# A decoder layer on one core: attention's output projection ahead of the convolution's, and a modulation set summed by VectorE

## The chip, the core and the metric

The kernel runs on one core of a Trainium2 chip. Five engines work side by side and meet at semaphores: TensorE (PE: matmuls and transposes), VectorE (DVE), ScalarE (ACT), GpSimd (POOL) and SyncE (SP, which only issues DMAs here). Matmuls write into eight PSUM banks; all else lives in SBUF. The metric is the device time of one execution in microseconds, the median of the runs. All data are float32 unless a row says bf16.

## The reference

```python
def reference(x, c, ...):                      # x: 1 x 256 x 1024
    mod = silu(c) @ w_ada + b_ada              # six vectors of 1024
    shift1, scale1, gate1, shift2, scale2, gate2 = split(mod)
    h = rms_norm(x) * (1 + scale1) + shift1
    x = x + gate1 * mixer(h)
    h = rms_norm(x) * (1 + scale2) + shift2
    return x + gate2 * moe(h)                  # top 4 of 32 experts, clamped SwiGLU

def mixer(h):
    u_conv, q, k, v, g = split(h @ w_in)       # 2048, 1024, 1024, 1024, 2048 columns
    y_conv = swish(layer_norm(causal_conv31(glu(u_conv)))) @ w_conv_out + b_conv_out
    o = diff_attention(rope(rms(q)), rope(rms(k)), v)     # 8 heads, two softmaxes each
    y_attn = rms_norm(o) * (1 - lam_init) @ w_attn_out
    g_conv, g_attn = split(sigmoid(g + b_gate))
    return (g_conv * y_conv + g_attn * y_attn) @ w_o
```

## The kernel before

There is no scheduler: each engine has its own program, and the order of work is the order in which its code is written. 256 tokens are two tiles of 128, 1024 channels are eight tiles of 128.

**Projections.** Weights come as blocks of 2 MB (128 x 4096) into a ring of six slots; the list `blocks` sets their order, and SP loads block n when block n-6 has been used (`used`, line 452). TensorE projects the convolution's columns, then q and k (`proj`, line 1281, eight tiles of 8 matmuls of 512 columns), then v (four tiles). The six modulation vectors come in three sets: the first (shift1, scale1) opens the kernel; the second and third (`ADA0`, four blocks of w_ada each, `ada_rows`, line 1194, 32 matmuls a set) stand before q/k and before v. Their rows are turned into columns at line 1316 (`mod2T`), and VectorE copies them out (lines 953, 955).

**Convolution.** VectorE runs the 31 taps of eight channel tiles in pairs (`conv`, line 864: a round is one tap of both tiles of a pair, two operations of 128x256). Rounds fill the time between other work: five rounds behind each of the eight q/k tiles (`between`), 28 operations and more behind them, the last ones inside heads 0 and 1. The LayerNorm follows inside the heads: sums over channels by VectorE (lines 997, 1001), mean and variance by a matmul against ones (`MEAN_AT` = 2, `VAR_AT` = 4). ScalarE's sigmoids (line 719, head 5) and GpSimd's products (lines 562, 565) make the swish.

**Heads.** q and k tiles are transposed (line 1327) and copied out by ScalarE (line 675). Per head h TensorE does the scores (lines 1360, 1364), half a gate tile (line 1288), the transposes of head h-1's probabilities (`turn`, line 1339), the other half, and head h-1's product with v (`attend`, lines 1349 to 1351). VectorE takes maxima (line 973), ScalarE the exponentials (line 698), VectorE the differences of the two softmaxes (lines 985, 986); ScalarE copies the transposed probabilities (line 681).

**Behind the heads.** Three blocks of the convolution's output projection (`y_conv`, line 1288), the transposes of the normalised heads (`oT`, line 1406; ScalarE copies them, line 729), the fourth y_conv block, four of attention's (`y_attn`), w_o (line 1426), the router, and then the expert units: a unit is up to 32 tokens of one expert, and 47 units run here. Every block here is 16 matmuls of 256 columns.

**Banks.** Banks 0 to 3 rotate: the list `order` gives every use a number, use n lies in bank n mod 4 (`bank`), and TensorE waits until use n-4 has been read out (`fill`).

**Expert weights.** 192 chunks of 2 MB go round eleven slots. The first eleven chunks take slots that the projections and tiles give up (`SLOT_ORDER`, `load_chunk`, lines 462 to 483); each later one waits for its slot's chunk to be used by a unit. GpSimd meanwhile splits the experts' biases into three bf16 pieces (lines 550 to 555), which are ready before the first unit.

## Time and profile before

| | us |
|---|---|
| median of 3 runs (1286.76 to 1287.35) | 1286.91 |
| the profiled execution | 1286.41 |
| its span, first to last instruction | 1284.6 |
| busy: TensorE matmuls / weight loads | 1080.6 / 528.3 |
| busy: VectorE / ScalarE / GpSimd | 404.4 / 219.0 / 51.7 |
| chain that ended last: PE / DMA / SP's queue | 49% / 41% / 5% |
| read from HBM: 473 MB, over the span | 369 GB/s |

The rows further down come from two views. A timeline row is a run of equal instructions: start, time from its first start to its last end, engine, line, operation, what it writes and reads, how many, and in brackets how long the engine had been idle and what released it. float32 matmuls and transposes stand as two records each. A windows row gives the busy time of each engine in one stretch, TensorE's granted clock as a share of its full 2.4 GHz, the DMA engines' busy share and GB/s.

### The profile page before, as it was taken

The page shows a single profiled execution, that of the slowest core. Times are in us where ns is not written, and L with a number is a line of the kernel's source. Part 1 is how long each engine was busy: PE and PEld are TensorE (multiplying, and loading weights), DVE is VectorE, ACT ScalarE, POOL GpSimd, SP SyncE. Part 2 cuts the span into 40 slices and gives each one's busy share as a digit, 9 for nine tenths or more (in the row PEclk, how much of TensorE's full clock was granted, in tenths as well). Part 3 has the DMA queues.
Part 4 walks back from the last instruction along what each step waited for, and adds up shares of the span by engine and source line. Part 5 has one row for each costly group of instructions (what it writes and reads, how often), then busy time and mean ns, then how long its engine had stood idle before and what let it go on. Part 6 is the DMA issues. An engine that isn't in the chain of part 4 may idle for free.

```text
span 1284.6 us, 23431 instructions
## 1 busy us (share of the span) xinstructions
PE 1080.6 (84%) x9958; PEld 528.3 (41%) x9958; DVE 404.4 (31%) x1129; ACT 219.0 (17%) x461; POOL 51.7 (4%) x91
## 2 busy tenths in 40 slices
PE   8999999899998566669998657968669696999975
PEld 5864458788433122224443212423224242444431
DVE  1388997631232111112222111212112121232221
ACT  1111124640121000002211001201002110122110
POOL 2000000355000000000000000000000000000000
PEclk9999999999999887889999888989889898999998
DMA  9998672256879999999999999999999999599997
GB/s 328 349 371 327 239 285 92 106 181 228 325 323 427 428 427 428 427 427 429 426 429 427 427 428 427 426 425 429 428 427 429 425 429 427 241 429 428 428 426 312
DMA packets 66084, 475.81 MB, mean 370 GB/s; under 512 B 6329, under 2 KB 19966, under 8 KB 39390
## 3 DMA queue, kind: packets, MB, share of 16 engines
q1 hardware_dynamic: 62100, 471.36, 89.2%
q0 software_dynamic: 816, 1.84, 0.5%
q10 hardware_dynamic: 3098, 1.56, 0.5%
q8 instruction: 59, 0.97, 0.3%
q14 instruction: 11, 0.09, 0.0%
HBM read 473.03 MB, written 1.05 MB: 369 GB/s over the span
## 4 chain that ended last, share of the span: by engine, by line
PE 49%; DMA 41%; SPq 5%; ACT 3%; DVE 1%; another core or an unknown queue 1%; issue 1%; ACTq 0%; DVEq 0%
DMA weights<-in_w_down 27%; PE bank L1556 14%; DMA weights<-in_w_up 13%; PE bank L1288 7%; PE bank L1584 7%; PE bank L1281 6%; SPq L462 4%; PE bank L1273 2%; PE bank L1426 2%; PE bank L1498 2%; PE bank L1224 2%; PE bank L1485 1%; PE bank L1194 1%; DMA weights<-in_w_ada 1%; PE bank L1505 1%
## 5 line engine op out<-in xcount | busy, mean ns | idle before, releaser
L1556 PE MATMUL bank<-weights,buf_d 128*32 128x512 f32 x3008 | 394.6, 671 | 141.6 <-DMA weights<-in_w_up 141.6
L1556 PEld LDWEIGHTS bank<-weights,buf_d 128*32 128x32 f32 x3008 | 96.9, 117 | 405.0 <-DMA weights<-in_w_up 211.5
L1584 PE MATMUL bank<-weights,buf_d 128*32 128x256 f32 x3008 | 177.6, 382 | 42.7 <-DMA weights<-in_w_down 39.9
L1165 DVE TENSOR_SCALAR u_conv<-bank 128x256 f32<-128x256 f32 x47 | 20.0, 425 | 467.5 <-PE bank L1556 467.5
L774 ACT ACTIVATE u_conv<-u_conv 128x256 f32<-128x256 f32 x47 | 19.6, 416 | 708.5 <-DVE u_conv L1165 708.5
L1584 PEld LDWEIGHTS bank<-weights,buf_d 128*32 128x32 f32 x3008 | 90.7, 110 | 115.5 <-DMA weights<-in_w_down 51.6
L864 DVE SCALAR_TENSOR_TENSOR weights<-u_conv,weights 128x256 f32<-128x256 f32 x240 | 97.8, 481 | 0.5
L1281 PE MATMUL bank<-weights,buf_d 128*128 128x512 f32 x192 | 82.9, 594 | 0.0
L1177 DVE TENSOR_TENSOR buf_d<-bank,u_conv 128x256 f32<-128x256 f32 x47 | 20.0, 425 | 180.1 <-PE bank L1584 180.1
L774 ACT ACT_TABLE_LOAD x47 | 60.3, 1283 | 1.4 <-issue 0.5
L1288 PE MATMUL bank<-buf_d,weights 128*128 128x256 f32 x256 | 58.6, 383 | 0.0
L1498 PE MATMUL bank<-buf_d 32*128 32x256 f32 x768 | 57.7, 416 | 0.6 <-DVE buf_d L1177 0.6
L1498 PEld LDWEIGHTS bank<-buf_d 32*128 32x128 f32 x768 | 36.4, 194 | 49.0 <-issue 47.6
L1288 PE MATMUL bank<-weights 128*128 128x256 f32 x256 | 55.6, 379 | 0.0
L1281 PEld LDWEIGHTS bank<-weights,buf_d 128*128 128x128 f32 x192 | 36.4, 190 | 46.6 <-issue 46.6
L1288 PEld LDWEIGHTS bank<-weights 128*128 128x128 f32 x256 | 48.6, 190 | 6.4
L1288 PEld LDWEIGHTS bank<-buf_d,weights 128*128 128x128 f32 x256 | 47.5, 190 | 8.4 <-issue 2.6
L1485 PE MATMUL bank<-x_tok,u_conv 128*32 128x256 f32 x768 | 50.1, 380 | 0.0
L1491 PE MATMUL bank<-ident,buf_d 128*128 128x128 f32 x190 | 38.2, 308 | 0.2 <-ACT buf_d L767 0.2
L1505 PE MATMUL bank<-late,u_conv 96*32 96x256 bf16 (+1 forms) x376 | 33.7, 343 | 0.5 <-DVE buf_d L1127 0.5
L1491 PEld LDWEIGHTS bank<-ident,buf_d 128*128 128x128 f32 x190 | 29.9, 204 | 4.4 <-ACT buf_d L767 0.3
L1158 DVE TENSOR_SCALAR u_conv<-u_conv 128x128 f32<-128x128 f32 x94 | 28.3, 344 | 6.8 <-issue 1.3
(274 smaller groups left out, 799.4 us busy)
## 6 DMA issues: line engine op xcount, KB each, us to landing
weights<-in_w_up SPq DMA_DIRECT2D x128, 2048.0 KB, 35.5
weights<-in_w_down SPq DMA_DIRECT2D x64, 2048.0 KB, 39.2
weights<-in_w_in SPq DMA_DIRECT2D x10, 2048.0 KB, 15.5
weights<-in_w_ada SPq DMA_DIRECT2D x8, 2048.0 KB, 19.3
weights<-in_w_ada SPq DMA_DIRECT2D x8, 1024.0 KB, 11.3
weights<-in_w_in SPq DMA_DIRECT2D x8, 512.0 KB, 10.1
weights<-in_w_in SPq DMA_DIRECT2D x4, 1024.0 KB, 13.1
weights<-in_w_conv_out SPq DMA_DIRECT2D x2, 2048.0 KB, 11.3
```

The lines of the kernel that those rows point to most:

```text
L462: sp.dma_start(dst, src).then_inc(w_full[chunk_slot(e, j)], 16)
L774: s.activation(sg, glu, ACT.Sigmoid, scale=ALPHA).then_inc(sg_ready, 1)
L864: ins = v.scalar_tensor_tensor(acc, u_conv[:, k, w:w + T], tap(k, w), acc, ALU.mult, ALU.add)
L1158: ins = v.tensor_scalar(pickw[:, tt, :], place_s.rearrange("p a s -> p (a s)"), upos[:, tt, bass.ds(u, 1)], uwt[:, tt, bass.ds(u, 1)], ALU ...
L1281: ins = t.matmul(bank(use)[:, :], lhsT[:, k, P * tt:P * tt + P], blk(n)[:, k, :], start=(k == 0), stop=(k == KD - 1))
L1288: ins = t.matmul(bank(use)[:, T * j:T * j + T], blk(n)[:, k, at:at + P], rhs[:, k, :], start=(k == 0), stop=(k == KD - 1))
L1485: ins = t.matmul(GX[SLOTS * g:SLOTS * g + SLOTS, 0:T], pick[:, tt, :], x_tok[:, tt, T * g:T * g + T], start=(tt == 0), stop=(tt == TT - 1))
L1491: ins = t.transpose(bank_[:, at + P * r:at + P * r + P], src.rearrange("p (c r) -> p r c", r=2)[:, r, :], ident[:])
L1498: ins = t.matmul(Y[q][:, T * tt:T * tt + T], Cmb[rows, P * tt:P * tt + P], oe[rows, :], start=False, stop=True, skip_group_check=True)
L1505: t.matmul(bank_[SLOTS * g:SLOTS * g + SLOTS, 0:width], sel, rows(g), start=True, stop=False)
L1556: ins = t.matmul(UP[SLOTS * g:SLOTS * g + SLOTS, :], xgT[:, r, SLOTS * j:SLOTS * j + SLOTS], up_group(w[:, r, :], g), start=False, stop=(j ...
L1584: ins = t.matmul(DOWN[rows, 0:T], actT[:, r, at:at + SLOTS], w[:, g, r, T * q:T * q + T], start=False, stop=(h == 1 and g == 1 and r == 1))
```

## The change

The third modulation set moves. Its four w_ada blocks are now loaded behind the gate blocks, and TensorE no longer multiplies them: behind the heads VectorE multiplies each of the eight 128x2048 pieces by its value of silu(c) and adds the sum so far (`mod_product`), and TensorE sums the result over partitions with four matmuls against ones (`sum_rows`), between the third and fourth y_attn block. Its columns (`turn_rows(1)`) follow the fourth.

Behind the heads the order is now oT, y_attn, then y_conv. Gate tile h-1 stands beside head h (before: gate tile h), so that none stands in head 0 and the last comes behind the last head. The swish's sigmoids leave the heads and follow the copies of oT. A q or k tile is followed by four rounds of taps instead of five; heads 0 to 3 hold 4, 5, 5 and 3 rounds, and the LayerNorm's mean and variance move from heads 2 and 4 to heads 4 and 6. The order of blocks, chunks and slots follows. The bias row of the third set is loaded straight into its place in `modrow2`.

```diff
-MEAN_AT, VAR_AT = 2, 4
+MEAN_AT, VAR_AT = 4, 6
...
-SLOT_ORDER = (0, VALUE_SLOT, 1, HEAD_SLOT, 2, 3, CONV_SLOT, GATE_SLOT, 4, 5, SMALL_SLOT)
+SLOT_ORDER = (VALUE_SLOT, 0, 1, 2, 3, CONV_SLOT, GATE_SLOT, HEAD_SLOT, 4, 5, SMALL_SLOT)
...
         blocks += [block_of(w_in, NB * i) for i in range(4, 8)]
-        ADA0[1] = len(blocks)
-        blocks += [ada_block(8 * NB, i) for i in range(4)]
         V0 = len(blocks)
         blocks += [block_of(w_in, NB * i) for i in range(8, 10)]
         GATE0 = len(blocks)
         blocks += [block_of(w_in, NB * i) for i in range(10, 14)]
+        ADA0[1] = len(blocks)
+        blocks += [ada_block(8 * NB, i) for i in range(4)]
+        AOUT0 = len(blocks)
+        blocks += [block_of(w_attn_out, 0), block_of(w_attn_out, NB)]
         COUT0 = len(blocks)
         blocks += [block_of(w_conv_out, 0), block_of(w_conv_out, NB)]
-        AOUT0 = len(blocks)
-        blocks += [block_of(w_attn_out, 0), block_of(w_attn_out, NB)]
...
-        order += [("ada", 1)] + [("v", i) for i in range(4)] + [("mod2T", 0), ("mod2T", 1)] + [("qkT", i) for i in range(8)]
-        for h in range(HEADS + 1):
-            if h < HEADS:
-                order += [("gate", h)]
-            if h:
-                order += [("aT", h - 1), ("o", h - 1)]
+        order += [("v", i) for i in range(4)] + [("mod2T", 0)] + [("qkT", i) for i in range(8)]
+        for h in range(1, HEADS):
+            order += [("gate", h - 1), ("aT", h - 1), ("o", h - 1)]
...
-        order += [("y_conv", i) for i in range(3)] + [("oT", i) for i in range(4)] + [("y_conv", 3)]
-        order += [(name, i) for name in ("y_attn", "w_o") for i in range(4)]
+        order += [("aT", HEADS - 1), ("o", HEADS - 1), ("gate", HEADS - 1)]
+        order += [("oT", i) for i in range(4)] + [("y_attn", i) for i in range(3)] + [("ada", 1), ("y_attn", 3), ("mod2T", 1)]
+        order += [("y_conv", i) for i in range(4)] + [("w_o", i) for i in range(4)]
...
-            for gi in range(2):
-                used[ADA0[gi] + i] = (ada_done, 3 * gi + i + 1)
+            used[ADA0[0] + i] = (ada_done, i + 1)
+            used[ADA0[1] + i] = (mod_summed, 2 * i + 3)
...
-            sp.wait_ge(*used[COUT0])
+            full(sp, OT_USE + 3)
             load_chunk(0, 0)
-            full(sp, OT_USE + 3)
-            load_chunk(0, 1)
-            sp.wait_ge(*used[COUT0 + 1])
-            load_chunk(0, 2)
-            sp.wait_ge(ebias_ready, 3 * PARTS)
-            load_chunk(0, 3)
             for i in range(2):
                 sp.wait_ge(*used[AOUT0 + i])
-                load_chunk(0, 4 + i)
-            full(sp, YA_USE + 3)
+                load_chunk(0, 1 + i)
+            for i in range(2):
+                sp.wait_ge(*used[COUT0 + i])
+                load_chunk(0, 3 + i)
+            full(sp, YC_USE[3])
+            load_chunk(0, 5)
+            sp.wait_ge(mixed, 4)
             load_chunk(1, 0)
-            sp.wait_ge(mixed, 4)
+            sp.wait_ge(ebias_ready, 3 * PARTS)
             load_chunk(1, 1)
...
+                    for gi in range(2):
+                        pool.wait_ge(bank_full[M2T_USE[gi] % 4], M2T_USE[gi] // 4 + 1)
                 pool.wait_ge(in_eb, 48 * (piece + 1))
...
-            for i in range(2):
-                s.activation(gates[:, KD * i:KD * i + KD, :], gates[:, KD * i:KD * i + KD, :], ACT.Sigmoid).then_inc(gate_ready, 1)
+            keep_gate(HEADS - 1)
             for i in range(4):
                 full(act_e, OT_USE + i)
...
+            sigmoid_gates(KD)
+            act_e.wait_ge(ln_ready, 1)
+            for k in range(KD):
+                s.activation(u_conv[:, k, 0:T], conv_acc[:, k, :], ACT.Sigmoid, scale=cols[:, 8 + k:9 + k],
+                             bias=cols[:, 16 + k:17 + k]).then_inc(sw_sig, 1)
+            sigmoid_gates(0)
...
+            def mod_product(k):
+                w, seen = (blk(ADA0[1] + j // 2, 2)[:, j % 2, :] for j in (k, max(k - 1, 0)))
+                if k % 2 == 0:
+                    dve.wait_ge(blk_full[place(ADA0[1] + k // 2)], 16 * loads_before[ADA0[1] + k // 2])
+                if k:
+                    dve.wait_ge(mod_summed, k)
+                    ins = v.scalar_tensor_tensor(w, w, c_act[:, k, 0:1], seen, ALU.mult, ALU.add)
+                else:
+                    ins = v.tensor_scalar(w, w, c_act[:, 0, 0:1], None, ALU.mult)
+                ins.then_inc(mod_summed, 1)
...
-            between = ([(1, 8, 13)], [(1, 13, 18)], [(1, 18, 23)], [(1, 23, 28)], [(1, 28, TAPS), (2, 0, 2)],
-                       [(2, 2, 7)], [(2, 7, 12)], [(2, 12, 17)])
+            between = ([(1, 8, 12)], [(1, 12, 16)], [(1, 16, 20)], [(1, 20, 24)], [(1, 24, 28)],
+                       [(1, 28, TAPS), (2, 0, 1)], [(2, 1, 5)], [(2, 5, 9)])
...
-            ada_row(1)
-            conv(2, 17, TAPS)
-            conv(3, 0, 11)
+            conv(2, 9, TAPS)
+            conv(3, 0, 8)
...
-            conv(3, 11, 19)
+            conv(3, 8, 14)
...
-                if h < 2:
-                    conv(3, (19, 26)[h], (26, TAPS)[h])
+                if h < 4:
+                    conv(3, (14, 18, 23, 28)[h], (18, 23, 28, TAPS)[h])
...
+            for k in range(4):
+                mod_product(k)
+            dve.wait_ge(gate_ready, 1)
+            for i in range(4):
+                use = YA_USE[i]
+                full(dve, use)
...
+                if i < 2:
+                    mod_product(2 * i + 4)
+                    mod_product(2 * i + 5)
+                if i == 2:
+                    ada_row(1)
...
+            def sum_rows():
+                use = ADA_USE[1]
+                fill(pe, use)
+                pe.wait_ge(mod_summed, KD)
+                total = blk(ADA0[1] + 3, 2)[:, 1, :]
+                for gi in range(4):
+                    ins = t.matmul(bank(use)[32 * gi:32 * gi + 32, :], ones[:, 0:32], total[:, NB * gi:NB * gi + NB],
+                                   start=True, stop=True)
+                ins.then_inc(bank_full[use % 4], 1)
...
-                channels(gate_use(h), n, par, 1, h1T)
-                if h:
+                    gate_half(h - 1, 1)
                     attend(h - 1)
...
-            conv_out(3)
             for i in range(4):
                 pe.wait_ge(bank_free[(OT_USE + i) % 4], (OT_USE + i) // 4 + 1)
             for i in range(4):
                 if i % 2 == 0:
                     wait_block(AOUT0 + i // 2)
-                fill(pe, YA_USE + i)
+                if i == 3:
+                    sum_rows()
+                fill(pe, YA_USE[i])
                 for j in range(2):
-                    channels(YA_USE + i, AOUT0 + i // 2, i % 2, j, oT)
...
+            turn_rows(1)
+            pe.wait_ge(swish_ready, KD)
+            for i in range(4):
+                conv_out(i)
```

TensorE from the last projection tile to the first scores, before (bank numbers shown; `late` is `modrow2`, the rows of the second and third set; line 1316 turns them, line 1327 transposes q and k tiles):

```order
L1316 MATMUL bank2<-ident,late 128x128 x4
L1316 MATMUL bank3<-ident,late 128x128 x4
L1327 MATMUL bank0<-ident,weights 128x128 x4
L1327 MATMUL bank1<-ident,weights 128x128 x4
L1327 MATMUL bank2<-ident,weights 128x128 x4
L1327 MATMUL bank3<-ident,weights 128x128 x4
```

And now (line 1343 turns the rows, line 1366 transposes):

```order
L1311 MATMUL bank0<-weights,buf_d 128x512 x8
L1343 MATMUL bank1<-ident,late 128x128 x4
L1366 MATMUL bank2<-ident,weights 128x128 x4
L1366 MATMUL bank3<-ident,weights 128x128 x4
L1366 MATMUL bank0<-ident,weights 128x128 x4
L1366 MATMUL bank1<-ident,weights 128x128 x4
```

One group of turned rows is left, and the fourth transposed tile now takes its bank, bank 1; before, the third and fourth took the banks of the two groups.

TensorE from the last head on, before (line 1339 is `turn`, 1349 to 1351 `attend`, 1288 a block or gate tile, 1406 oT, 1426 w_o):

```order
L1339 MATMUL bank<-ident,weights 128x128 x3
L1349 MATMUL bank<-weights 128x128
L1350 MATMUL bank<-weights 128x128
L1351 MATMUL bank<-weights 128x128
L1288 MATMUL bank<-weights 128x256 x48
L1406 MATMUL bank<-ident,weights 128x128 x16
L1288 MATMUL bank<-weights 128x256 x80
L1426 MATMUL bank<-weights,buf_d 128x512 x32
```

And now (line 1318 is a block or gate tile, 1447 oT, 1353 `sum_rows`, 1343 the turned rows, 1472 w_o):

```order
L1378 MATMUL bank<-ident,weights 128x128 x3
L1388 MATMUL bank<-weights 128x128
L1389 MATMUL bank<-weights 128x128
L1390 MATMUL bank<-weights 128x128
L1318 MATMUL bank<-buf_d,weights 128x256 x16
L1447 MATMUL bank<-ident,weights 128x128 x16
L1318 MATMUL bank<-weights 128x256 x48
L1353 MATMUL bank<-weights 32x512 x4
L1318 MATMUL bank<-weights 128x256 x16
L1343 MATMUL bank<-ident,late 128x128 x4
L1318 MATMUL bank<-weights 128x256 x64
L1472 MATMUL bank<-weights,buf_d 128x512 x32
```

The last gate tile stands behind the last head, oT directly behind it, and the summed and turned rows stand among the blocks; the matmuls of the third set are gone from the projections.

VectorE from the last head's copies on, before (line 1013 normalises the heads, 1031 multiplies y_conv, 1040 y_attn, 1042 adds both):

```order
L964 COPY weights<-bank 128x2x128 x2
L1012 RECIPROCAL weights<-weights 128x16
L1013 TENSOR_TENSOR weights<-weights 128x2048
L1021 TENSOR_TENSOR weights<-weights 128x256
L1022 TENSOR_REDUCE weights<-weights 128x32
L1023 TENSOR_TENSOR weights<-weights 1x32
L1024 TENSOR_TENSOR weights<-weights 128x256
L1031 SCALAR_TENSOR_TENSOR weights<-bank,weights 128x256 x8
L1040 TENSOR_TENSOR weights<-weights,bank 128x512
```

And now (line 1029 normalises, 854 and 852 are the products, 1040 multiplies y_attn, 844 adds the bias row):

```order
L980 COPY weights<-bank 128x2x128 x2
L1028 RECIPROCAL weights<-weights 128x16
L1029 TENSOR_TENSOR weights<-weights 128x2048
L854 TENSOR_SCALAR weights<-weights 128x2048
L852 SCALAR_TENSOR_TENSOR weights<-weights 128x2048 x3
L1040 TENSOR_TENSOR weights<-weights,bank 128x512
L852 SCALAR_TENSOR_TENSOR weights<-weights 128x2048 x2
L1040 TENSOR_TENSOR weights<-weights,bank 128x512
L852 SCALAR_TENSOR_TENSOR weights<-weights 128x2048 x2
L1040 TENSOR_TENSOR weights<-weights,bank 128x512
L844 TENSOR_TENSOR late<-bank,late 128x512
L1040 TENSOR_TENSOR weights<-weights,bank 128x512
```

Eight products stand behind the normalised heads, four ahead of the first y_attn block's result and two behind each of the first two; the router's weights (lines 1021 to 1024 before) moved behind the mixing.

## Rows read from the trace of the kernel before

**Rows 1.** Windows: length, PE, PEld, DVE, ACT, POOL busy; clock, DMA share, GB/s.

```profile
180.00:260.00 80.00, 75.37 (x420) 61.95 (x418) 56.90 (x141) 42.20 (x132) 13.02 (x22) 1.00 0.31 111
260.00:324.00 64.00, 63.09 (x305) 55.04 (x304) 15.73 (x26) 12.84 (x22) 29.89 (x31) 1.00 0.64 218
...
364.00:1262.00 898.00, 717.83 (x8052) 284.49 (x8040) 188.64 (x556) 125.05 (x230) 0.00 (x0) 0.92 0.99 420
```

**Rows 2.** Timeline (start us, us, what), SP's DMA issues around the first unit.

```profile
362.76 4.06 SPq L462 DMA_DIRECT2D weights<-in_w_down  x2
```

**Rows 3.** Timeline, TensorE, 144 to 187 us; in brackets idle time before.

```profile
144.44 7.07 PE L1194 MATMUL bank<-weights 128*32 128x512 f32 x64
...
179.02 1.11 PE L1316 MATMUL bank<-ident,late 128*128 128x128 f32 x8
179.96 3.66 PE L1327 MATMUL bank<-ident,weights 128*128 128x128 f32 x32
184.87 0.49 PE L1360 MATMUL bank<-weights 128*128 128x384 bf16 x2 [1.25 <-ACT weights L675]
...
186.14 7.17 PE L1288 MATMUL bank<-buf_d,weights 128*128 128x256 f32 x32
```

**Rows 4.** Timeline, VectorE, a q/k tile's reductions and the first head.

```profile
105.44 0.68 DVE L924 TENSOR_REDUCE weights<-weights 128x8 f32<-128x512 f32 x1
...
113.20 0.68 DVE L924 TENSOR_REDUCE weights<-weights 128x8 f32<-128x512 f32 x1
...
186.70 1.14 DVE L973 TENSOR_REDUCE weights<-bank 128x1 f32<-128x128 f32 x4
...
187.96 5.75 DVE L864 SCALAR_TENSOR_TENSOR weights<-u_conv,weights 128x256 f32<-128x256 f32 x14
...
195.47 1.14 DVE L973 TENSOR_REDUCE weights<-bank 128x1 f32<-128x128 f32 x4
```

**Rows 5.** Timeline, TensorE, inside the heads.

```profile
193.57 0.93 PE L1364 MATMUL bank<-weights 64*128 64x128 f32 x8
...
197.98 0.49 PE L1339 MATMUL bank<-ident,weights 128*128 128x128 f32 x3
...
202.21 0.39 PE L1351 MATMUL bank<-weights 128*128 128x128 f32 x2
...
202.85 0.93 PE L1364 MATMUL bank<-weights 64*128 64x128 f32 x8
...
221.21 0.39 PE L1351 MATMUL bank<-weights 128*128 128x128 f32 x2
...
231.62 0.46 PE L1349 MATMUL bank<-weights 128*128 128x128 f32 x2 [1.41 <-ACT weights L681]
...
242.61 0.46 PE L1349 MATMUL bank<-weights 128*128 128x128 f32 x2 [1.04 <-ACT weights L681]
```

**Rows 6.** Timeline, TensorE, behind the heads up to w_o.

```profile
265.24 20.89 PE L1288 MATMUL bank<-weights 128*128 128x256 f32 x96
285.96 1.91 PE L1406 MATMUL bank<-ident,weights 128*128 128x128 f32 x16
...
322.24 27.63 PE L1426 MATMUL bank<-weights,buf_d 128*128 128x512 f32 x64
```

**Rows 7.** Timeline, ScalarE's copies of transposed heads, and VectorE's 128x2048 product.

```profile
286.60 2.42 ACT L729 ACTIVATE weights<-bank,weights 128x512 f32<-128x512 f32 x4 [13.89 <-PE bank L1406]
...
268.00 2.29 DVE L1013 TENSOR_TENSOR weights<-weights 128x2048 f32<-128x2048 f32 x1
```

**Rows 8.** Timeline, TensorE among the expert units, and windows with the granted clock.

```profile
420.68 1.92 PE L1556 MATMUL bank<-weights,buf_d 128*32 128x512 f32 x16 [1.56 <-DMA weights<-in_w_up]
425.58 3.56 PE L1556 MATMUL bank<-weights,buf_d 128*32 128x512 f32 x16 [2.97 <-DMA weights<-in_w_up]
...
426.00:428.00 2.00, 2.00 (x12) 0.40 (x8) 0.00 (x0) 0.00 (x0) 0.00 (x0) 0.50 0.94 401
```

**Rows 9.** Timeline, VectorE beside GpSimd's swish.

```profile
253.54 0.76 DVE L986 SCALAR_TENSOR_TENSOR weights<-weights 128x128 f32<-128x128 f32 x1
```

## What I expect

> **What bounds the kernel now.** I read the stretches first [rows 1]. Up to 364 us TensorE is busy nearly throughout (75.37 of 80 us and 63.09 of 64 in the two stretches shown) while the DMA engines stand at shares of 0.31 and 0.64. From 364 to 1262 us it is the other way round: DMA share 0.99 at 420 GB/s for 898 us, TensorE 717.83 us busy. So the expert weights' stream sets the end, and it can't run at full rate before the first unit frees a slot: the eleventh chunk is issued at 362.76 [rows 2] and finds the engines idle. Whatever moves the first unit moves the end by as much; a load that is shifted about inside the first 364 us costs nothing as long as it lands in time. The path to the first unit is TensorE's, in four pieces: the projections up to 179.02 [rows 3], the opening of the heads, which VectorE sets (the first scores end at 186.14, VectorE's first maximum starts at 186.70, right behind its taps) [rows 3, 4], the heads themselves [rows 5], and nine dense blocks behind them up to the w_o projection at 322.24 [rows 6]. From there on the change alters nothing that TensorE waits for, so the start of w_o is what I forecast.
>
> **The opening of the heads.** Removed from TensorE: 32 matmuls of the third modulation set, 7.0 us from 144.44 [rows 3], and half of the turned rows (8 records from 179.02 to 179.96, so 0.47). The value tiles thus end at 172.0 instead of 179.02. This gain isn't kept, because VectorE is not ready. Its work ahead of the first maximum shrinks by ten taps (14 of pair 3's rounds done instead of 19) and one 128x512 addition: 14 taps took 5.75 us, 0.41 each, and a 128x512 operation 0.68 [rows 4], together 4.1 + 0.65. It doesn't idle on the way: a q or k tile costs it 7.76 us now (105.44 to 113.20), 6.95 with two taps fewer, and TensorE delivers one in 6.91, as any block of that size (three from 265.24 to 285.96) [rows 4, 6]. So VectorE opens the heads at 186.70 - 4.75 = 182.0.
>
> TensorE gets a new wait ahead of that. The fourth transposed q/k tile now has the bank of the second modulation set's columns. VectorE frees that bank by a copy, which stands 12 taps ahead of the opening: 182.0 - 4.9 = 177.1. TensorE arrives at 172.5 + 3 x 0.46 = 173.9 and waits 3.2 us; behind it are queued five tiles and the first scores. From 179.96 to 184.87 eight tiles and ScalarE's copies took 4.91 us [rows 3]; five of them take 3.5, so the scores start at 180.6 and end at 181.9 (184.87 to 186.14 is 1.3). It is just hidden: VectorE and scores meet at 182.0.
>
> **The heads.** With no gate tile in front of head 0, VectorE's chain decides. Its first head took 8.77 us (186.70 to 195.47) with 14 taps [rows 4]; with 8 it is 6.3. From the turned probabilities to the last matmul of attend(0) TensorE takes 4.2 (197.98 to 202.21) [rows 5]. attend(0) thus falls at 182.0 + 6.3 + 4.2 = 192.5, against 202.21: 9.7 us earlier, having done one gate tile (6.91) less. Then four periods of 9.28 (193.57 to 202.85) with the mean's matmul, 0.44 (the 19.00 from 202.21 to 221.21 is two periods and it): attend(4) at 230.1. VectorE's 17 rounds of taps fit: a head with ten taps takes it about 7.5 us. What delayed heads 3 and 4, the sums for the LayerNorm, comes two heads later with the same length: 10.41 (221.21 to 231.62) and 10.99 (to 242.61) [rows 5], so attend(6) starts at 251.5. The last head has no gate tile beside it, so VectorE's 1.8 us for the probabilities (193.7, the taps' end, to 195.47), the turn, ScalarE's copy and the attend lie bare: 3.3 by my estimate from those pieces, ending at 254.8. Before it was 265.24: 10.4 us ahead.
>
> **Behind the heads.** Before: three blocks, the transposes at 285.96 (1.75 by the blocks around them: 36.28 us to 322.24 less five of 6.91) and five blocks, 57.0 us in all [rows 6]. Now nine blocks, since gate(7) stands here: + 6.91. The transposed heads are copied by ScalarE, 2.42 us from 286.60 [rows 7], and were covered by a block; now y_attn needs them at once, and ScalarE must first empty gate(7)'s bank (two halves, 0.9 by estimate from those copies). TensorE waits till 3.5 us after the transposes began instead of 1.75: + 1.75. The summed rows are 4 of the 32 matmuls that took 7.0: + 0.9, and their turn + 0.5. Together 67.0, so 10.0 us are given back.
>
> VectorE's eight products hide. A 128x2048 operation takes it 2.2 us (2.29 at 268.00) [rows 7]; it starts when the normalised heads are done, 5.0 us behind the last attend (265.24 to 270.3). Four are done 14 us behind it, ahead of the first y_attn block at 17.3; two more behind each of the next blocks end at about 29.5, and TensorE asks at 31.1. If that cover goes, TensorE waits for the rest, and y_attn(3), the turn and all convolution blocks with it. SP's queue: the convolution's and w_o's blocks now wait for products (the last for the summed rows), and the first expert chunk stands behind them, at about 287 instead of behind the second convolution block at 279. ScalarE's queue issues four more small bias loads at about 63 us, where it waits for TensorE anyway. The last two chunks ahead of the units wait for w_o tiles in both kernels, so nothing reaches the first unit. GpSimd's swish (the 13.02 us of the first stretch [rows 1]) moves behind the heads: it starts some 14 us behind the last attend, when ScalarE's copies and first sigmoids are done, and the convolution's blocks begin at 39, so 12 us are to spare. Its bias pieces, now behind the second turn at about 295, are 30 us of work [rows 1] and some DMA waits, done some 20 us ahead of the units.
>
> **Sum.** - 10.4 + 10.0 = - 0.4 us at one clock. A cost is left that the trace shows elsewhere. The same 16 matmuls take 1.92 us behind a wait of 1.56 and 3.56 behind one of 2.97 [rows 8]: 1.64 lost, and the granted clock of the two us from 426 reads 0.50, the 1.2 GHz level, where it otherwise reads 1.00, 2.4 GHz. The new wait of 3.2 has only transposes around it, and the last heads have 2.5 us of small waits in 4.5. The bounds are no fall (0) and a fall at both and at y_attn's wait (4.9). I take one fall, most of it uncovered: + 1.4, because 3.2 is nearest to the row with 2.97.
>
> The Trainium skill ("TensorE: Matmul & The Clock Gate", section "Why this matters for your kernels") warns of idle gaps between bursts of matmuls as what sends the clock back to its lower level. By it the new wait alone makes the change a loss of 1.2 us; by the waits of 1.25 and 1.41 that this trace shows without a slow matmul behind them [rows 3, 5] it would stay at - 0.4. The measured waits lie on both sides, so the row decides.
>
> Total + 1.0: 1286.41 (the profiled execution: span 1284.6 and 1.8 around it) becomes 1287.4. The median of the runs lies 0.5 above that execution, so I predict 1287.9.
>
> **Rivals.** *The clock falls twice or three times* (slower). For it: three new places of waiting. Against: the waits before, up to 1.41 [rows 5], cost nothing. Price: 3.3 to 4.9 - 0.4, so 1289.8 to 1291.4 from the median of 1286.9; it decides once two falls are uncovered. *VectorE and GpSimd get into each other's way* (slower): the swish now runs beside the products. A 128x128 operation took 0.76 beside GpSimd's swish [rows 9], where taps of twice the size take 0.41. If four products wait 0.7 each, the eighth comes at 32.3 against 31.1, and each further delay counts in full; with the mixing beside the bias pieces I put 1 to 3 us: about 1290. The Trainium skill ("SBUF — State Buffer", section "SBUF: two separate sides") says that a VectorE operation with two SBUF inputs and a GpSimd operation exclude each other for a whole instruction. By it the swish waits too, up to 9 us for four products, which its 12 still cover. *The bare waits vanish* (faster): if ScalarE, without the sigmoids inside the loop, hides the LayerNorm sums, the periods of 10.41 and 10.99 fall towards 9.28 and nothing cools: - 0.4 - 2.7, so 1283.8 from that median. Against: VectorE, not ScalarE, carries those sums.
>
> **Chances.** Forecast 0.52, clock 0.24, port 0.08, bare waits gone 0.16. About 0.2% (2.6 us) is what a measurement can tell from no change; the forecast with its own error of 1.5 us stays inside it. The range runs from just below the faster rival to the dearer clock: 1283.5 to 1291.8. Faster 0.16, same 0.52, slower 0.32.
>
> **What would show it.** VectorE's first maximum at 182.0 and TensorE's wait of about 3 us inside the transposes; attend(0) near 192.5; the last attend near 255; a wait of 1.75 ahead of y_attn; no wait at the summed rows; w_o from 322 to 324; the granted clock of 1 us stretches at 178 to 183 and 250 to 262. It is wrong if VectorE opens the heads much before 181, if the heads keep another period, or if w_o starts with TensorE waiting for mixed halves.

## Result and profile after

The changed kernel takes 1293.45 us, the median of six runs (1291.70 to 1295.51), against 1287.48 for the kernel before in runs on the same chip (six, 1286.76 to 1287.75). The ratio is 1.0049, 95% interval 1.0037 to 1.0060: 6.0 us slower, and 1.65 above the upper end of the range. The profiled execution took 1295.39, its span is 1293.6 (1284.6 before), so it is 9.0 us longer; its own pieces are explained first, the medians by the experiments.

The stretches that answer to [rows 1], windows of after (length, TensorE, its weight loads, VectorE, ScalarE, GpSimd busy; granted clock, DMA share, GB/s):

```profile
180.00:260.00 80.00, 74.08 (x393) 59.84 (x392) 57.20 (x141) 34.80 (x124) 0.00 (x0) 0.95 0.22 80
260.00:330.00 70.00, 68.20 (x320) 58.24 (x320) 32.28 (x29) 15.74 (x25) 36.28 (x41) 0.99 0.84 292
```

GpSimd has nothing to do in the heads any more, and the granted clock is no longer 1.00 there. The opening of the heads, timelines of TensorE and of VectorE (start us, us, what, in brackets the idle time before and what ended it), and two windows:

```profile
177.90 4.53 PE L1366 MATMUL bank<-ident,weights 128*128 128x128 f32 x20 [3.59 <-DVE weights L972]
...
177.80 4.96 DVE L884 SCALAR_TENSOR_TENSOR weights<-u_conv,weights 128x256 f32<-128x256 f32 x12
185.72 1.15 DVE L989 TENSOR_REDUCE weights<-bank 128x1 f32<-128x128 f32 x4 [2.96 <-PE bank L1411]
...
178.00:180.00 2.00, 2.00 (x10) 2.00 (x11) 1.96 (x6) 0.68 (x2) 0.00 (x0) 0.50 0.56 238
184.00:186.00 2.00, 2.00 (x11) 1.06 (x10) 0.28 (x2) 0.35 (x1) 0.00 (x0) 0.50 0.04 8
```

The forecast wait is there, 3.59 us behind VectorE's copy at L972. Behind it the granted clock stands at 0.50, the 1.2 GHz level, through the transposes and the first scores. VectorE is ready at 182.76 (some 0.5 us of this comes from a fall of the clock near 20 us in this execution, far ahead of the change), and its first maximum starts 2.96 us later, at 185.72. The end of the heads and the way to w_o, TensorE's timeline:

```profile
255.60 0.46 PE L1388 MATMUL bank<-weights 128*128 128x128 f32 x2 [1.04 <-ACT weights L683]
257.20 0.52 PE L1378 MATMUL bank<-ident,weights 128*128 128x128 f32 x3 [0.70 <-DVE weights L1002]
258.38 0.69 PE L1388 MATMUL bank<-weights 128*128 128x128 f32 x2 [0.66 <-ACT weights L683]
...
259.72 8.14 PE L1318 MATMUL bank<-buf_d,weights 128*128 128x256 f32 x32
267.70 1.91 PE L1447 MATMUL bank<-ident,weights 128*128 128x128 f32 x16
271.41 20.96 PE L1318 MATMUL bank<-weights 128*128 128x256 f32 x96 [1.80 <-ACT weights L726]
292.30 1.07 PE L1353 MATMUL bank<-weights 128*32 128x512 f32 x8
...
328.40 27.63 PE L1472 MATMUL bank<-weights,buf_d 128*128 128x512 f32 x64
```

The clock falls a second time at these waits: the last gate tile lasts 7.98 us (259.72 to 267.70) where an undisturbed one lasts 6.91. w_o starts at 328.40 against 322.24 [rows 6], the first unit at 369.59 against 363.42, so 6.2 late. But the end is 9.0 late, and the other 2.8 us stand ahead of the first unit as well, in SP's queue. SP's timeline, expert chunks, and windows of the DMA engines:

```profile
331.79 0.33 SPq L461 DMA_DIRECT2D weights<-in_w_up  x1
356.91 1.41 SPq L461 DMA_DIRECT2D weights<-in_w_up  x3
368.93 2.96 SPq L461 DMA_DIRECT2D weights<-in_w_down  x2
...
350.00:356.00 6.00, 6.00 (x17) 2.66 (x16) 2.78 (x4) 0.72 (x2) 5.71 (x5) 1.00 0.00 0
362.00:369.00 7.00, 5.67 (x43) 2.71 (x41) 6.22 (x33) 2.67 (x10) 0.00 (x0) 1.00 1.00 426
```

The seventh chunk is asked for at 331.79, the eighth at 356.91, and the ninth and tenth right behind it, although w_o's blocks had freed their slots at about 349 and 356 (20.8 and 27.7 us behind the start of w_o, as bias_chunk_last shows below). The DMA engines move nothing from 350 to 356. SP stands at its wait for GpSimd's bias pieces, whose buffer lies in the eighth chunk's slot. In the kernel before the same wait stands ahead of the fourth chunk and ends at 312.65, long before w_o's slots come free, so it holds none of the last chunks there. GpSimd's timeline of after, and behind it the last row of the same chain in the kernel before:

```profile
274.96 0.55 POOL L558 TENSOR_SCALAR weights<-weights 128x256 f32<-128x256 f32 x1 [264.10 <-ACT u_conv L737]
...
293.26 1.68 POOL L567 DMA_DIRECT2D weights<-in_b_up  x3
307.27 1.03 POOL L548 CAST late<-weights 96x1024 bf16<-96x1024 f32 x1 [6.24 <-DMA u_conv<-late]
327.98 1.03 POOL L548 CAST late<-weights 96x1024 bf16<-96x1024 f32 x1 [10.96 <-DMA weights<-in_b_up]
349.25 1.03 POOL L548 CAST late<-weights 96x1024 bf16<-96x1024 f32 x1 [11.26 <-DMA weights<-in_b_down]
354.75 2.13 POOL L553 TENSOR_TENSOR late<-weights,late 32x1024 bf16<-32x1024 f32 x1
...
310.18 2.45 POOL L555 TENSOR_TENSOR late<-weights,late 32x1024 bf16<-32x1024 f32 x1
```

The pieces end at 356.88 instead of 312.63. Three chunks of 2.097 MB at the 427 GB/s of the units take 14.7 us, so the stream catches up at 371.6, 2.7 us after SP wants to send the eleventh.

### The profile page after: what moved, and what is told of

Read it like the earlier page. It is cut to its first block, busy times and chain, and to the rows that moved or that the text cites. A ratio compares the mean times of both kernels' runs of the same rounds, so it can differ in the third digit from the quotient of the medians.

```text
span 1293.6 us, 23338 instructions
## 1 busy us (share of the span) xinstructions
PE 1087.4 (84%) x9902; PEld 531.3 (41%) x9902; DVE 426.3 (33%) x1137; ACT 216.8 (17%) x459; POOL 59.9 (5%) x91
## 4 chain that ended last, share of the span: by engine, by line
PE 42%; DMA 39%; DVE 8%; SPq 6%; ACT 2%; another core or an unknown queue 1%; issue 1%; ACTq 0%; DVEq 0%
DMA weights<-in_w_down 27%; PE bank L1602 13%; DMA weights<-in_w_up 12%; PE bank L1318 7%; PE bank L1630 7%; SPq L461 6%; DVE weights L884 4%; PE bank L1254 2%; PE bank L1303 2%; PE bank L1472 2%; PE bank L1544 2%; PE bank L1531 1%; PE bank L1551 1%; DMA weights<-in_b_ada 1%
## 5 line engine op out<-in xcount | busy, mean ns | idle before, releaser
L1207 DVE TENSOR_TENSOR buf_d<-bank,u_conv 128x256 f32<-128x256 f32 x47 | 20.0, 425 | 179.8 <-PE bank L1630 179.8
L1318 PE MATMUL bank<-buf_d,weights 128*128 128x256 f32 x256 | 59.5, 387 | 0.0
L1254 PE MATMUL bank<-buf_d,weights 128*128 128x256 f32 x128 | 30.7, 398 | 1.2 <-ACT buf_d L623 1.2
```

What stands on the lines that cost most here:

```text
L1254: ins = t.matmul(PS[4 + k][:, T * half:T * half + T], first_conv(i)[:, kk, half, P * k:P * k + P], h1T[:, 2 * i + kk, :], start=False, sto ...
L1318: ins = t.matmul(bank(use)[:, T * j:T * j + T], blk(n)[:, k, at:at + P], rhs[:, k, :], start=(k == 0), stop=(k == KD - 1))
```

## Experiments

Before they ran, two causes stood against each other and against a third: the queue (SP's wait for the bias pieces), the clock (its falls at TensorE's new waits), and work that the prediction had called hidden (products and swish). This table has the profiled execution of each kernel in us (first maximum, start of w_o, issue of the eighth chunk, first unit, span) and, outside the profile, the median of its runs with the ratio to the kernel before, measured beside it. Chunk 8 is `load_chunk(1, 1)`, wherever it stands in the queue. In the kernels made from after the bias pieces lie in its slot; in before and taps_and_norm_late they lie in the fourth chunk's, which is asked for at 312.65 and 326.99.

| kernel | max. | w_o | chunk 8 | unit | span | median | ratio (95%) |
|---|---|---|---|---|---|---|---|
| before | 186.7 | 322.2 | 323.9 | 363.4 | 1284.6 | 1286.7 to 1287.5 | |
| after | 185.7 | 328.4 | 356.9 | 369.6 | 1293.6 | 1293.45 | 1.0049 (1.0037-1.0060) |
| bias_chunk_last | 183.6 | 326.1 | 354.2 | 367.3 | 1288.7 | 1290.84 | 1.0031 (1.0019-1.0044) |
| bank_freed_early | 182.1 | 326.2 | 355.7 | 367.4 | 1292.5 | 1293.42 | 1.0046 (1.0032-1.0060) |
| busy_before_bank | 182.7 | 325.2 | 354.0 | 366.4 | 1291.3 | 1291.25 | 1.0033 (1.0021-1.0045) |
| busy_tail | 182.1 | 323.1 | 351.2 | 364.2 | 1289.5 | 1292.99 | 1.0042 (1.0028-1.0056) |
| short_products | 184.8 | 327.5 | 355.9 | 368.7 | 1292.4 | 1294.61 | 1.0055 (1.0042-1.0069) |
| bias_piece_early | 183.3 | 332.1 | 339.8 | 373.4 | 1297.9 | 1296.68 | 1.0067 (1.0054-1.0081) |
| both_repaired | 182.0 | 323.0 | 351.6 | 364.2 | 1285.3 | 1287.78 | 1.0007 (0.9998-1.0016) |
| taps_and_norm_late | 186.6 | 337.0 | 338.6 | 378.3 | 1300.9 | 1301.23 | 1.0107 (1.0092-1.0122) |
| opening_best | 179.8 | 322.4 | 351.6 | 363.6 | 1284.9 | 1286.72 | 0.9998 (0.9989-1.0007) |
| opening_gate0 | 180.5 | 321.1 | 351.2 | 362.5 | 1283.8 | 1286.56 | 0.9993 (0.9984-1.0002) |
| opening_v3 | 179.6 | 319.3 | 348.2 | 360.7 | 1282.0 | 1284.21 | 0.9982 (0.9973-0.9990) |

**bias_chunk_last.** SP's order alone:

```diff
-            sp.wait_ge(ebias_ready, 3 * PARTS)
-            load_chunk(1, 1)
             for i in range(2):
                 sp.wait_ge(*used[WO0 + i])
                 load_chunk(1, 2 + i)
+            sp.wait_ge(ebias_ready, 3 * PARTS)
+            load_chunk(1, 1)
```

> SP asks for the eighth expert chunk, whose slot GpSimd's bias pieces occupy, behind the ninth and tenth instead of ahead of them; nothing else differs from the changed kernel. Theory 'queue' (three chunk loads stood behind SP's wait for the bias pieces until 356.9 us, so the stream was 8.9 us late where the first unit was 6.2 us late): the ninth chunk is issued near 349, the tenth near 356, the DMA engines stand idle again ahead of the first unit, first unit to end is 921 us as in the kernel before, and the time is 2.7 us less than the changed kernel's, about 1290.7. Rival 'the units themselves got slower' (clock inside them): first unit to end stays 924, about 1293.5.

SP's timeline and a window of this kernel:

```profile
346.93 7.67 SPq L461 DMA_DIRECT2D weights<-in_w_up  x3
366.64 2.99 SPq L461 DMA_DIRECT2D weights<-in_w_down  x2
...
350.00:356.00 6.00, 5.84 (x26) 3.58 (x25) 1.74 (x3) 1.74 (x4) 3.48 (x3) 1.00 0.87 317
```

The transfers go on from 350 to 356, and first unit to end is 921.4 us (1288.7 - 367.3) against 921.2 before and 924.0 in after. The median falls by 2.6. The queue is shown, at its expected price. The table says it a second way: in the five kernels with the changed order of SP whose eighth chunk is late (after, bank_freed_early, busy_before_bank, busy_tail, short_products) first unit to end is 923.7 to 925.3 us, in the five with the eighth chunk last 921.1 to 921.4. What the stream hangs on shows at the 121st chunk. Those first five ask for it 537.8 to 538.2 us behind the eighth chunk, a spread of 0.4, but 525.1 to 526.1 behind the first unit; the other five ask for it 522.4 to 522.7 behind the first unit, as the kernel before does (522.6).

**bank_freed_early.** VectorE's copy moved:

```diff
-            conv(3, 0, 8)
+            conv(3, 0, 3)
...
             v.tensor_copy(by_chunk[:, 0, :, :, :], columns(0, 2)).then_inc(bank_free[M2T_USE[0] % 4], 1)
-            conv(3, 8, 14)
+            conv(3, 3, 14)
```

> VectorE copies the second modulation set's columns behind the third tap round of the last pair (about 173.5 us) instead of behind the eighth; the number of taps ahead of the heads is the same. Theory 'clock' (TensorE's wait of 3.59 us among the transposes let the granted clock fall, and transposes and scores at half rate made VectorE wait 2.96 us): no wait among the transposes, VectorE's first maximum near 182.8 instead of 185.7, time about 1290.5. TensorE then waits some 4 us ahead of the first turned probabilities; if the clock falls there instead, up to 3 us come back: 1293.5. Rival 'VectorE opens the heads late whatever TensorE does': first maximum still at 185.7, 1293.5.

The wait and the fall among the transposes are gone and the first maximum is at 182.07. TensorE now runs out of work at the other side. Its timeline:

```profile
188.69 0.87 PE L1378 MATMUL bank<-ident,weights 128*128 128x128 f32 x3 [5.28 <-DVE weights L1002]
189.36 4.77 PE L1318 MATMUL bank<-buf_d,weights 128*128 128x256 f32 x16
```

The gate half lasts 4.60 us up to 193.96 instead of 3.45: the fall has moved behind the new wait of 5.28, which the expectation had allowed for. w_o still starts 2.2 us ahead of after (326.19), but the eighth chunk comes only 1.2 earlier, and the median is that of after.

**busy_before_bank.** Work in the wait, the wait itself left:

```diff
+                if i == 3:
+                    pe.wait_ge(lo_free, 4)
+                    for k in range(14):
+                        t.matmul(PS[4 + k % 4].rearrange("p (a c) -> p a c", a=4), identb[:],
+                                 maskb[:, P:2 * P].unsqueeze(1).to_broadcast([P, 4, P]), start=True, stop=True,
+                                 skip_group_check=True)
                 fill(pe, use)
```

> Fourteen matmuls of 128x512 that nobody reads, 0.21 us each, are put on TensorE ahead of its wait for the bank of the modulation columns; the wait's end (VectorE's copy near 177.7 us) is the same. Theory 'clock': the bank comes at the same time, the remaining transposes take 2.3 us instead of 4.5 and the scores 1.3 instead of 2.4, VectorE's first maximum near 182.8, time about 1290.5. Rival 'the wait alone, not the clock, makes the scores late': transposes and scores as long as before, first maximum near 185.7, 1293.5.

Timelines of TensorE and VectorE:

```profile
174.06 3.19 PE L1363 MATMUL bank<-weights 128*128 128x512 bf16 x14
177.83 2.40 PE L1372 MATMUL bank<-ident,weights 128*128 128x128 f32 x20 [0.59 <-DVE weights L972]
...
182.70 1.15 DVE L989 TENSOR_REDUCE weights<-bank 128x1 f32<-128x128 f32 x4
```

The bank comes at the same moment (177.83 against 177.90), the same twenty transposes take 2.40 instead of 4.53, and VectorE no longer waits. So the loss at the opening was the clock and not the wait. The median falls by 2.2, but the runs overlap (1290.05 to 1293.05 against 1291.70 to 1295.51), so the size is rough; both_repaired gives a firmer one.

**busy_tail.** The same matmuls at the end of the heads; `busy(h, count)` issues them into head h's score banks, once its exponentials are done:

```diff
                     gate_half(h - 1, 1)
+                    if h >= 6:
+                        busy(h - 1, 4)
                     attend(h - 1)
...
+            busy(HEADS - 2, 4)
             turn(HEADS - 1)
+            busy(HEADS - 2, 3)
             attend(HEADS - 1)
```

> Matmuls of 128x512 that nobody reads stand in TensorE's four waits at the end of the heads (four ahead of attend(5) and attend(6) each, four ahead of the last turn, three ahead of the last attend, 0.21 us each); everything else as in the changed kernel. Theory 'clock': the fall near 253 to 258 that all five profiles show is gone, the last gate tile takes 6.9 to 7.0 instead of 7.9 to 8.4, and the end comes 1.0 to 1.4 earlier: about 1292.2. Rival 'those matmuls only fill the queue and delay the turn': no gain or up to 1 us slower, 1293.5 to 1294.5.

TensorE's timeline:

```profile
177.21 2.40 PE L1366 MATMUL bank<-ident,weights 128*128 128x128 f32 x20 [3.58 <-DVE weights L972]
...
255.46 7.07 PE L1318 MATMUL bank<-buf_d,weights 128*128 128x256 f32 x32
262.37 1.91 PE L1458 MATMUL bank<-ident,weights 128*128 128x128 f32 x16
```

The last gate tile is back at 6.91 (255.46 to 262.37), as in all four kernels with these matmuls; in all eight others but the kernel before the clock fell between 252 and 265. The median gains 0.5, less than the spread of these runs (2.0), so the size of the effect on the end rests on the profile. This execution had no fall at the opening either, although TensorE waited 3.58 us there with nothing to do: of the five profiles with that wait unfilled and as long, four show the fall, of different lengths, and this one none. At the same clock throughout, w_o starts at 323.07: the changed work costs 0.8 there, not 6.2.

**short_products.** The products cut to a sliver:

```diff
-                w, seen = (blk(ADA0[1] + j // 2, 2)[:, j % 2, :] for j in (k, max(k - 1, 0)))
+                w, seen = (blk(ADA0[1] + j // 2, 2)[:, j % 2, 0:8] for j in (k, max(k - 1, 0)))
```

> VectorE's eight products of the third modulation set are cut to the first 8 of 2048 columns (the set is then not summed over its rows, and the output differs for that reason); all waits stay. If the products are hidden, as the prediction said, TensorE's wait ahead of the summed rows stays at nothing and the time stays at 1293.5 (1292.5 to 1294), although GpSimd's swish beside them gets shorter (18.3 us there, 10.6 in the kernel before), since GpSimd then waits for the summed rows at 294. Rival 'products and swish get into each other's way and that is what is lost': 1 to 3 us faster, 1290.5 to 1292.5.

GpSimd's timeline:

```profile
284.43 1.68 POOL L567 DMA_DIRECT2D weights<-in_b_up  x3
294.24 1.97 POOL L574 DMA_DIRECT2D u_conv<-late  x4 [8.13 <-DVE late L844]
```

The swish beside them shrinks from 18.3 us (274.96 to 293.26) to 10.4, and GpSimd then waits 8.13 for the summed rows: the same step comes 0.9 earlier, as expected, and the kernel isn't faster: 1294.61, somewhat above the 1292.5 to 1294 that were expected. Products and swish do get into each other's way, but under cover.

**bias_piece_early.** A second lever on the queue: GpSimd's program starts with the b_down piece ahead of the swish (`bias_loads` and `bias_parts` are the old loop's body as two functions; the other two pieces follow where they stood).

```diff
+            pool.wait_ge(sc_full, HEADS)
+            bias_loads(2)
+            bias_parts(0, 2)
             for k in range(KD):
                 pool.wait_ge(sw_sig, k + 1)
```

> The changed kernel with SP's order as it is; GpSimd does the third of its bias pieces (b_down) before the swish, in the time in which it waits for ScalarE's sigmoids anyway, instead of last. A second lever on the same wait. Theory 'queue': the pieces are done near 336 instead of 356.9, so SP's wait no longer holds the ninth chunk (which is free near 349), first unit to end is 921 us instead of 924, and the time falls by 2.7 as it did with the chunk order: about 1290.8. Rival 'the gain of the other order came from the order of the transfers, not from the wait': 1293.5 as before.

The first half came true: the eighth chunk is asked for at 339.83, the ninth at 352.86, right behind w_o's tiles, and at the 121st chunk the stream is again as far behind the first unit as in the kernel before, within 0.1 us. The time did not, 1296.68. GpSimd's timeline, then VectorE's in the last head, then TensorE's:

```profile
252.08 2.12 POOL L549 TENSOR_TENSOR weights<-weights,late 96x1024 f32<-96x1024 f32 x1
254.27 2.12 POOL L552 CAST late<-weights 32x1024 bf16<-32x1024 f32 x2
256.47 2.11 POOL L553 TENSOR_TENSOR late<-weights,late 32x1024 bf16<-32x1024 f32 x1
...
252.88 1.35 DVE L1003 TENSOR_SCALAR weights<-weights 128x2 f32<-128x2 f32 x1
254.26 1.11 DVE L1008 TENSOR_SCALAR weights<-weights 128x128 f32<-128x128 f32 x1
255.41 1.12 DVE L1009 SCALAR_TENSOR_TENSOR weights<-weights 128x128 f32<-128x128 f32 x1
256.46 2.28 DVE L1008 TENSOR_SCALAR weights<-weights 128x256 f32<-128x256 f32 x1
...
259.40 0.87 PE L1385 MATMUL bank<-ident,weights 128*128 128x128 f32 x3 [5.34 <-DVE weights L1009]
```

In after the same four operations take 0.23, 0.29, 0.35 and 0.35. Beside GpSimd's pieces each ends just behind an operation of GpSimd's, TensorE waits 5.34 instead of 0.70, and the clock is low from 256.4 to 266.6. The Trainium skill ("SBUF — State Buffer", section "SBUF: two separate sides") says that of two operations which need the port pair that VectorE and GpSimd share, the second blocks for the first one's whole instruction; the trace agrees, with 1.35 and 2.28 us beside operations of 2.1, and 1.1 beside each of the two casts that take 2.12 together.

Some 3 us more of this execution's lateness arise late, between the 161st and the 162nd chunk, where SP waits for TensorE's units: 61.15 us pass there, 59.61 in busy_tail, 58.2 to 58.4 in the other eleven kernels. TensorE's timelines of bias_piece_early and of busy_tail there:

```profile
1098.83 3.08 PE L1637 MATMUL bank<-weights,buf_d 128*32 128x256 f32 x32 [3.83 <-DMA weights<-in_w_down]
...
1090.83 3.28 PE L1641 MATMUL bank<-weights,buf_d 128*32 128x256 f32 x32 [2.72 <-DMA weights<-in_w_down]
```

Both show one more fall of the clock behind a wait for a transfer; the same 32 matmuls take 1.93 in the other kernels. short_products waits 2.70 at the same place without a fall and loses nothing. So the 1.4 us of busy_tail are the clock, and the 2.9 here the clock and the longer wait.

**both_repaired.** bias_chunk_last, busy_before_bank and busy_tail in one kernel.

> The changed kernel with the eighth chunk last on SP's queue and unread matmuls both ahead of the transposes' bank wait and in the four waits at the end of the heads; taps, heads and all other orders as changed. If the queue and the clock are the two causes and nothing else is: no fall between 170 and 265 us, first unit near 364.2 (0.8 behind the kernel before, as in the one profile without a fall there), first unit to end 921.3, time about 1287.8, so half of what remains of the forecast of +1.0 in ratio: 1.0006. If a third cause is left: above 1289.

The median is 1287.78, as expected, with a ratio whose interval holds 1. All the change's own edits are in it but the eighth chunk's place in SP's queue. Queue and clock thus account for 5.7 of the 6.0 us (by the ratios, for 0.0042 of 0.0049); singly they gave 2.6 + 2.2 + 0.5 = 5.3. Against bias_chunk_last, which has the queue's repair alone, the kernel gains 3.1, and the runs of the two don't overlap (1286.87 to 1289.64 and 1289.94 to 1292.38): that is the clock. The rows of TensorE that the point-by-point part below uses:

```profile
177.14 2.40 PE L1372 MATMUL bank<-ident,weights 128*128 128x128 f32 x20 [0.56 <-DVE weights L972]
...
255.41 7.07 PE L1318 MATMUL bank<-buf_d,weights 128*128 128x256 f32 x32
262.32 1.91 PE L1464 MATMUL bank<-ident,weights 128*128 128x128 f32 x16
266.04 20.96 PE L1318 MATMUL bank<-weights 128*128 128x256 f32 x96 [1.81 <-ACT weights L726]
323.03 7.46 PE L1489 MATMUL bank<-weights,buf_d 128*128 128x512 f32 x17
```

**taps_and_norm_late.** The change's tap rounds and LayerNorm places in the kernel before (`between` as changed, too):

```diff
-MEAN_AT, VAR_AT = 2, 4
+MEAN_AT, VAR_AT = 4, 6
...
-            conv(2, 17, TAPS)
-            conv(3, 0, 11)
+            conv(2, 9, TAPS)
+            conv(3, 0, 8)
...
-            conv(3, 11, 19)
+            conv(3, 8, 14)
...
-                if h < 2:
-                    conv(3, (19, 26)[h], (26, TAPS)[h])
+                if h < 4:
+                    conv(3, (14, 18, 23, 28)[h], (18, 23, 28, TAPS)[h])
```

> A part alone: the kernel before with the changed kernel's tap rounds (four per q and k tile, 14 of the last pair ahead of the heads, the rest behind four maxima) and with its later LayerNorm sums (heads 4 and 6 instead of 2 and 4); projections, modulation sets and queues as before. VectorE is ready about 4 us earlier but the scores, which TensorE ends at 186.1, are not, so nothing is gained at the opening. The swish comes some 18 us later: its sigmoids now stand in the last head ahead of ScalarE's copy for attend(7), GpSimd's part runs into the first convolution block, and SP's wait for the bias pieces ends near 331 instead of 313 with five chunks behind it. Expected 1293 to 1297. If lateness of the swish and of the pieces cost nothing: 1286.5.

TensorE's timeline:

```profile
268.92 0.77 PE L1349 MATMUL bank<-weights 128*128 128x128 f32 x2 [5.31 <-ACT weights L681]
...
277.76 22.46 PE L1288 MATMUL bank<-weights 128*128 128x256 f32 x93 [7.22 <-POOL weights L565]
```

1301.23, dearer than the expected 1293 to 1297: TensorE waits 5.31 us behind the sigmoids in ScalarE's last head and 7.22 for the swish, with the clock low in between. The first unit is 14.9 late, so SP's wait hardly shows (first unit to end 922.6). With the convolution's output projection still ahead of attention's, moving the taps and the LayerNorm thus costs 14.5 us; in the changed kernel the other order behind the heads makes room for the late swish.

**opening_best, opening_gate0, opening_v3.** Three steps towards a faster kernel. The first has SP's order of bias_chunk_last, the copy behind the third round, and 11 instead of 14 rounds of the last pair ahead of the heads (4, 6, 6 and 4 behind the first maxima). The second adds the tail's matmuls and the whole first gate tile ahead of `turn(0)`; the third lets ScalarE copy that turn first. Their own lines, in this order:

```diff
+            conv(3, 3, 11)
...
+                    conv(3, (11, 15, 21, 27)[h], (15, 21, 27, TAPS)[h])
...
+                    if h == 1:
+                        gate_half(0, 1)
                     turn(h - 1)
-                    gate_half(h - 1, 1)
+                    if h > 1:
+                        gate_half(h - 1, 1)
...
+                if h == 1:
+                    keep_aT(0)
                 act_e.wait_ge(s_max, h + 1)
...
+                if h > 1:
+                    keep_aT(h - 1)
                 if h:
-                    keep_aT(h - 1)
```

> The eighth chunk last on SP's queue, the modulation columns copied early, and three of the tap rounds ahead of the heads moved into the heads (4, 6, 6 and 4 rounds behind the first four maxima). If both theories hold: VectorE ready near 180.3 and scores done near 180, first maximum near 180.4 (5.3 us ahead of the changed kernel), heads at the same period, 2.7 us less in the stream: about 1285.4, ahead of the kernel before by 2. If the clock falls ahead of the first turned probabilities, or twelve taps in a head lengthen its period of 9.28: 1287 to 1288. If neither theory holds: 1293.

> The version with the early copy, the eighth chunk last and three tap rounds moved, plus two edits: both halves of the first gate tile ahead of the first turn (TensorE waits 2.93 us there in that version), and the unread matmuls at the end of the heads. If TensorE's bare time is what is left: the first turn still near 186.7, attend(0) near 188.5 instead of 191.0, no fall at the tail: 2 + 1.2 us ahead of that version's 1286.7, about 1283.5. If VectorE becomes the bound of the heads behind the earlier start (twelve taps in heads 1 and 2), the 2 us are lost again by head 3: 1285.5.

> The last version (early copy, eighth chunk last, three tap rounds moved, first gate tile whole ahead of the first turn, unread matmuls at the end of the heads), with ScalarE copying the first turned probabilities ahead of the second head's exponentials instead of behind them (TensorE waited 2.52 us for that copy ahead of attend(0)). Expected: attend(0) near 189.3 instead of 191.3, the same 9.28 per head after it, first unit near 360.5, about 1284.6, ratio near 0.998. If the later exponentials of the second head delay its turn instead (12 taps stand in that head): attend(1) is back near 200.5 and the time is that of the last version, 1286.6.

TensorE's timeline at the first turn and attend(0), a row of each kernel in this order:

```profile
186.38 0.52 PE L1378 MATMUL bank<-ident,weights 128*128 128x128 f32 x3 [2.93 <-DVE weights L1002]
...
190.49 0.46 PE L1388 MATMUL bank<-weights 128*128 128x128 f32 x2 [2.52 <-ACT weights L683]
...
187.76 0.46 PE L1391 MATMUL bank<-weights 128*128 128x128 f32 x2 [0.66 <-ACT weights L683]
```

opening_best reached 1286.7, not 1285.4. Its profile still has the tail's fall, but opening_gate0, whose profile has none, is no faster in the median, so the reason isn't shown. opening_gate0 missed its 1283.5 by 3 us: filling the wait of 2.93 uncovered another of 2.52, for ScalarE's copy behind the second head's exponentials. opening_v3 takes that away: attend(0) ends at 188.7, w_o starts at 319.3, and with 1284.21 (ratio 0.9982, 0.9973 to 0.9990) it is faster than both kernels, 2.5 us ahead of the kernel before.

## Why the prediction was wrong

*What bounds the kernel* held: the stream sets the end, and the time ahead of the units moves it. But "whatever moves the first unit moves the end by as much" was too narrow. The end hangs on the later of two things, the first unit and the arrival of the ten chunks asked for ahead of it.

*The opening, at one clock,* held closely. In both_repaired the transposes go on at 177.14 (forecast 177.1) and the first maximum starts at 182.02 (182.0). The wait of 3.2 was 3.59.

*The heads* held: in both_repaired the last matmul of attend(0) starts at 192.90 (192.5), the period is 9.28, the LayerNorm's delays stand two heads later with 10.42 and 10.99 (10.41 and 10.99), the heads end at 255.4 (254.8).

*Behind the heads* held nearly: gate(7) 6.91, y_attn 3.72 behind the transposes (3.5), y_attn to w_o 56.99 (56.6 from the forecast's own terms). 67.6 us against 67.0. The products are hidden: TensorE meets no wait at the summed rows in after, and short_products isn't faster.

*The sum at one clock* was - 0.4 at w_o; it is + 0.8 (323.03 against 322.24), by small errors of one sign.

*The clock term* was mis-sized. I took one fall at 1.64, mostly uncovered, + 1.4, from a row among the units, where 16 matmuls in a row run slow [rows 8]. Here the slow stretch lay over a chain: transposes, ScalarE's copies, scores, and VectorE behind them, 2.96 us of bare waiting in the profiled execution, and 1.46 in the shorter fall of bias_chunk_last. A second fall, at the end of the heads, came in every profile of the changed heads that had no matmuls in those waits. In the medians the two are worth 2.2 and 0.5, so 2.7 (3.1 by both_repaired against bias_chunk_last). That was the first rival (two falls, 3.3 in its price), which had 0.24; by itself it would have stayed inside the range (1287.5 + 0.8 + 2.7 = 1291.0).

*The step that failed* is "nothing reaches the first unit", and with it the harmless GpSimd chain. I compared the pieces' end with the first unit ("some 20 us ahead"; it is 12.7) instead of with the moment at which SP needs it. SP's wait stands ahead of the ninth and tenth chunk, which I had looked at alone. The chain also ended later than I made it. Its first piece began at 307.27, behind the gate rows' DMAs, instead of at 295; in the kernel before, 14 us lie between the swish and the first piece for the same reason (256.88 to 270.94). And its loads waited 10.96 and 11.26 us where the same loads waited 8.61 and 6.15 before; beside them the DMA engines moved 364 GB/s from 300 to 330 us instead of 249. Done near 343, as forecast, the pieces would have met the ninth slot coming free at about the same time and cost next to nothing; done at 356.88 (351.6 in both_repaired, where the clock doesn't fall ahead of the units) they are late for it. Price 2.6 in the median, 2.8 in the profile. In place of + 1.0 the parts thus add up to 0.8 + 2.7 + 2.6 = 6.1, against 6.0 measured.

*The port rival* names a real effect with the wrong place: swish and products slow each other and it costs nothing there; beside the last head it would cost 4.6 us (5.34 against 0.70), as bias_piece_early shows, but the change puts nothing of GpSimd's there. *The bare waits* didn't vanish: the period of 11.0 and the waits of 1.42 and 1.04 stayed (and their price was 2.84 by the rows, 10.41 + 10.99 less two periods of 9.28, not 2.7).

One thing stays open: whether the runs of after spread more than those of before, and why. Six runs of after lie within 3.8 us; the six of before beside them lie within 1.0, but its 55 later runs within 4.4 (1286.02 to 1290.39). Falls that come or not at these waits would spread the runs, but only a profiled execution shows where the clock fell; of the others only the mean clock is known (0.928 to 0.944 for after).

## What to carry to other kernels

For each wait in a load queue, ask what is queued behind it and when *those* loads could have gone, not only when the waiting one is needed; a wait for a slow helper chain belongs behind the loads that wait for something earlier. Price a fall of the clock by the dependent chain that runs while it is low, and try some unread matmuls in a wait whose end is fixed. Filling one wait uncovers the next engine's order (here ScalarE's): look at who would be late next before counting the gain.

## What was not expected of the hardware

The length of a wait alone didn't decide whether the clock fell: it stayed at 1.00 behind 2.93 us ahead of `turn(0)` in opening_best and behind 3.58 at the opening in busy_tail, and fell at the end of the heads behind 1.04, 0.70 and 0.66 with a few 128x128 matmuls between them. With fourteen matmuls of 0.21 us inside the opening's wait it stayed at 1.00 in both profiles; without them it fell in four of five. VectorE's single-input operations (0.29 us) took as long as two-input ones (1.1) beside GpSimd's pieces, where I had expected only two-input ones to wait.
